# FFN up product of a hybrid decoder block: gate and up chunk computed together, block by block, in alternating pairs of PSUM banks

## What is computed

```python
def conv_ffn(xn, w_up, conv_w, conv_b, w_down):      # xn (1, 256, 2048), D_FF = 5632
    h = causal_dwconv(xn @ w_up, conv_w, conv_b)     # w_up (2048, 11264), 3 taps
    a, b = jnp.split(h, 2, axis=-1)                  # gate half, up half
    return (jax.nn.silu(a) * b) @ w_down             # w_down (5632, 2048)
```

## Time and profile before

| | |
|---|---|
| median of 3 runs | 1511.31 us (1510.9 to 1511.93) |
| the profiled execution's own time | 1510.21 us |
| its span, first to last instruction | 1508.4 us |
| mean granted clock of TensorE | 0.999 of full speed |
| PE matmuls busy | 1493.1 us (99%) |
| PE weight loads busy | 1280.1 us (85%) |
| DVE busy | 1076.9 us (71%) |
| ACT busy | 818.1 us (54%) |
| share of PE in the chain that ended last | 97% |
| weights and inputs read from HBM | 286.18 MB, 191 GB/s over the span |

### The profile page before, as it was taken

The page is one execution under the profiler, slowest core; times in us unless marked ns, Lnnn a source line. Parts: engine busy times, 40 slices in busy tenths (PEclk is TensorE's granted clock), DMA queues, the critical chain, the costliest instruction groups (busy, mean ns, idle before and its releaser), DMA issues.

```text
span 1508.4 us, 24165 instructions
## 1 busy us (share of the span) xinstructions
PE 1493.1 (99%) x7908; PEld 1280.1 (85%) x7908; DVE 1076.9 (71%) x1576; ACT 818.1 (54%) x1184; POOL 2.9 (0%) x9
## 2 busy tenths in 40 slices
PE   8999999999999999999999999999999999999997
PEld 6888888888888888888888888888888888888886
DVE  5756676788887556665568777777777777777876
ACT  5644478745555546544566454454545555454654
POOL 0000000000000000000000000000000000000000
PEclk9999999999999999999999999999999999999999
DMA  8756655665557554445546655655555556555554
GB/s 307 271 193 219 208 177 190 201 201 167 176 167 240 179 187 160 155 149 195 187 164 199 190 194 187 192 185 194 192 185 195 184 190 195 193 183 191 185 194 139
DMA packets 80314, 288.88 MB, mean 192 GB/s; under 512 B 8928, under 2 KB 10464, under 8 KB 79376
## 3 DMA queue, kind: packets, MB, share of 16 engines
q1 hardware_dynamic: 76320, 276.33, 56.0%
q10 hardware_dynamic: 3456, 8.64, 1.7%
q0 software_dynamic: 496, 3.34, 0.6%
HBM read 286.18 MB, written 2.10 MB: 191 GB/s over the span
## 4 chain that ended last, share of the span: by engine, by line
PE 97%; DVE 1%; ACT 1%; DMA 0%; issue 0%; SPq 0%; ACTq 0%; DVEq 0%
PE ps L261 96%; PE ps L318 0%; DMA raw<-in_stream 0%; DVE wlo L877 0%; ACT whi L527 0%; DVE vm L1354 0%; DVE xres L1364 0%; PE ps L390 0%; ACT scr L761 0%; ACT scr L854 0%; DVE sm_ L1223 0%; DVE xres L1327 0%; SPq L217 0%; DVE wlo L931 0%; ACT vm L867 0%
## 5 line engine op out<-in xcount | busy, mean ns | idle before, releaser
L261 PE MATMUL ps<-xT,whi 128*128 128x512 f32 x2304 | 727.5, 397 | 0.2
L877 DVE TENSOR_TENSOR wlo<-raw,whi 128x1024 fp32r<-128x1024 f32 x516 | 623.3, 1222 | 129.5 <-ACT whi L527 120.0
L527 ACT ACTIVATE whi<-raw 128x1024 fp32r<-128x1024 f32 x516 | 531.7, 1050 | 227.5 <-PE ps L261 220.9
L261 PEld LDWEIGHTS ps<-xT,wlo 128*128 128x128 f32 x2304 | 432.8, 188 | 102.1
L261 PE MATMUL ps<-whi,mixT 128*128 128x512 f32 x1472 | 461.1, 391 | 7.2 <-DVE wlo L935 5.8
L261 PE MATMUL ps<-xT,wlo 128*128 128x256 f32 x2304 | 453.0, 278 | 0.0
L261 PEld LDWEIGHTS ps<-xT,whi 128*128 128x128 f32 x2304 | 352.6, 189 | 2.3 <-DVE wlo L877 0.8
L261 PEld LDWEIGHTS ps<-whi,mixT 128*128 128x128 f32 x1472 | 277.3, 188 | 65.6 <-DVE mixT L926 5.8
L261 PE MATMUL ps<-wlo,mixT 128*128 128x512 f32 x736 | 287.2, 390 | 0.0
L542 ACT ACTIVATE hl<-ps 128x256 f32<-128x256 f32 x160 | 61.1, 382 | 236.7 <-PE ps L261 236.6
L895 DVE TENSOR_TENSOR tmp<-ps,hl 128x256 f32<-128x256 f32 x160 | 67.8, 424 | 146.1 <-ACT hl L542 145.8
(11 more groups left out here) (173 smaller groups left out, 637.4 us busy)
## 6 DMA issues: line engine op xcount, KB each, us to landing
raw<-in_stream SPq DMA_DIRECT2D x519, 512.0 KB, 3.4
xres<-in_xin ACTq DMA_DIRECT2D x2, 1024.0 KB, 6.9
scr<-in_xt_in ACTq DMA_DIRECT2D x8, 256.0 KB, 3.6
xres<-in_xin POOLq DMA_DIRECT2D x1, 2048.0 KB, 12.0
out_x<-vm SPq DMA_DIRECT2D x4, 512.0 KB, 3.1
kT<-in_memt_in SPq DMA_DIRECT2D x2, 512.0 KB, 8.7
vbuf<-in_memin ACTq DMA_DIRECT2D x1, 1024.0 KB, 9.4
gel<-in_memin ACTq DMA_DIRECT2D x1, 1024.0 KB, 7.4
```

The lines of the kernel that those rows point to most:

```text
L261: return nc.tensor.matmul(o, l, r, start=start, stop=stop, skip_group_check=True)
L527: A(whi[:, 2 * pr + s, :], raw[:, 2 * pr + s, :], ACT.Copy).then_inc(hi_done, 1)
L877: V.tensor_tensor(wlo[:, 2 * pr + s, :], raw[:, 2 * pr + s, :], f32(whi[:, 2 * pr + s, :]), ALU.subtract).then_inc(lo_done, 1)
```

## The change

The panels of a pair are laid out anew in the stream, so that slots 0 and 1 of its unit hold blocks kk = 0 to 7 of the gate chunk a and of the up chunk b, and slots 2 and 3 hold blocks 8 to 15 of a and b. PE goes through the blocks once for both chunks: at each kk it issues w_hi of a, w_hi of b, w_lo of a, w_lo of b against the same block of `xT`, and it waits for two panels at a time, before kk = 0 and before kk = 8. Pairs with even k accumulate in banks 4 and 5, those with odd k in banks 6 and 7. ACT and DVE now have nothing of the pair to do in the first of a unit's two steps; both copies, both sums and everything behind them are in the second. In the FFN's first pair `norm_tr(7)` stays at kk = 7, which is now late in the first half of the pair, and `row_of(2)` comes at kk = 13.

```diff
-            def up(m, n=2 * GF, at={}):
-                for j in range(n):
-                    narrow(m + j // 2, j % 2, xT, {} if j else at)
+            def up_pair(m, k, at={}):
+
+                for s in range(2):
+                    pe.wait_ge(lo_done, 4 * m + (2 * s + 2))
+                    for kk in range(8 * s, 8 * s + 8):
+                        if kk in at:
+                            at[kk]()
+                        w = slice(kk % 8 * P, (kk % 8 + 1) * P)
+                        for ab in range(2):
+                            mm(ps[:, 4 + 2 * (k % 2) + ab, :], whi[:, 2 * s + ab, w],
+                               xT[:, kk].rearrange("p a b -> p (a b)"), kk == 0, False)
+                        for ab in range(2):
+                            last = mm(ps[:, 4 + 2 * (k % 2) + ab, :T], wlo[:, 2 * s + ab, w], xT[:, kk, 0, :], False, kk == KT - 1)
+                            if kk % 8 == 7:
+                                last.then_inc(panels_used, 1)
...
-                    14: lambda: pe.wait_ge(nt_lo, 2 * KT)}
-            narrow(C_F // 2, 0, xT, NEXT)
-            narrow(C_F // 2, 1, xT, {7: lambda: row_of(2)})
-            up(C_F // 2 + 1, 2 * GF - 2)
+                    13: lambda: row_of(2), 14: lambda: pe.wait_ge(nt_lo, 2 * KT)}
+            up_pair(C_F // 2, 0, NEXT)
+            pe.wait_ge(row_read, 3)
+            for k in range(1, GF):
+                up_pair(C_F // 2 + k, k)
             with pe.Fori(1, NG - 1) as g:
                 m = C_F // 2 - 2 + 6 * g
-                up(m, 2)
+                up_pair(m, 0)
                 down(m + 1, g)
-                up(m + 3, 6)
-
-            up(NC // 2 - 8)
+                for k in range(1, GF):
+                    up_pair(m + 2 + k, k)
+
+            for k in range(GF):
+                up_pair(NC // 2 - 8 + k, k)
...
             def pair(m, g, k, hi_now, k0=0, also=None):
                 u, q = 8 * g + 2 * k, 4 * g + k
-                step(m, 0, lambda: copy_hl(0), lambda: last_tap(u, 0), lambda: (silu(q), also() if also else None))
-                step(m, 1, lambda: copy_hl(1), lambda: last_tap(u + 1, 1),
-                     (lambda: hidden_hi(q, k, k0)) if hi_now else None)
+
+                def both():
+                    for ab in range(2):
+                        A(hl[:, ab, :], ps[:, 4 + 2 * (k % 2) + ab, T:], ACT.Copy).then_inc(hl_copied, 1)
+
+                def rest():
+                    last_tap(u + 1, 1)
+                    silu(q)
+                    if hi_now:
+                        hidden_hi(q, k, k0)
+
+                step(m, 0, None, None, also)
+                step(m, 1, both, lambda: last_tap(u, 0), rest)
...
-            def up(u, ab, w):
-                ch.link(narrow_sum(w, ab, tmp[:, 5, :]))
-                V.tensor_tensor(tmp[:, ab, :], tmp[:, 5, :], row[:], ALU.mult).then_inc(up_ready, 1)
+            def up(u, ab, w, k):
+                dve.wait_ge(hl_copied, w + 1)
+                ch.link(V.tensor_tensor(tmp[:, 5 + ab, :], ps[:, 4 + 2 * (k % 2) + ab, :T], hl[:, ab, :], ALU.add))
+                V.tensor_tensor(tmp[:, ab, :], tmp[:, 5 + ab, :], row[:], ALU.mult).then_inc(up_ready, 1)
...
-                def up_a():
-                    if first:
-                        first()
-                    up(u, 0, w)
-
-                def b1():
+                def both():
+                    up(u, 0, w, k)
+                    up(u + 1, 1, w + 1, k)
+
+                def rest():
                     taps(u + 1, 1)
                     hidden(q, k)
-
-                step(m, 0, up_a, lambda: taps(u, 0))
-                step(m, 1, lambda: up(u + 1, 1, w + 1), b1, (lambda: hidden_lo(q, k, k0)) if lo_now else None)
+                    if lo_now:
+                        hidden_lo(q, k, k0)
+
+                step(m, 0, None, None, first)
+                step(m, 1, both, lambda: taps(u, 0), rest)
...
-    up = np.stack([up[:NF], up[NF:]], 1)
+    up = np.stack([up[:NF], up[NF:]], 1).reshape(NF, 2, P, 2, PAN).transpose(0, 3, 2, 1, 4).reshape(NF, 2, P, D)
```

## The result

The changed kernel takes **1521.38 us** (median of 4 runs, 1520.32 to 1521.81) against 1511.11 in the same comparison: 1.0068 times as long, 95% interval 1.0055 to 1.008. Forecast were 1520.3 us, between 1514 and 1527. The profiled execution took 1521.81 us with a span of 1520.0, against 1510.21 and 1508.4.

What follows compares the result with a forecast made beforehand. PE was taken to bound the kernel, waiting for nobody. Late panels (5.1 + 1.0) and the turn into the FFN (2.8) gave 8.9 us: 1519.1 on the profiled execution, median 1.1 higher, so 1520.3; 80% range 1514 to 1527.

Steps and rivals of the forecast that it cites:

- The pair's second step: ACT's and DVE's step behind a pair: slot 3 late by 0.19 us (loop) or 0.14 (written out); 5.1 plus 1.0 us.
- PE's own pace: PE's matmuls in the up product: 0 change taken, with bounds of 0.680 and 0.697 us a group.
- The rival that lives on them: Up product: repeating the moving operand in another bank brings groups to 0.680 us; total +1.7, 1513.0 us; chance 0.05.
- The second ladder: Chain from a pair's end to the next unit's slots 0 and 1: ready at 10.84, due 11.04, 0.20 us to spare.
- The turn: Entry into the FFN, first pair: PE stands 3.1 us once, 0.3 us is given back, net 2.8 us.
- The hole at slot 3: First FFN pair, before kk = 8: slot 3, split only after the last quarter's transposes, makes PE stand 3.1 us once.
- no wait before kk = 0: Sign for the FFN's pairs: PE does not wait for slots 0 and 1; waits there would make the prediction wrong.
- What was given back: First FFN pair: the wait ahead of `row_of(2)` goes, 0.3 us.
- The clock: Rival at the FFN's start: the 3.1 us hole brings the lower clock level, 2.4 us more, 1522.6 us; chance 0.07.
- that sign: Sign for PE: the profile's granted clock row still reads 1.00.
- The one that the Trainium skill has on cycling banks: Rival: the clock falls at each of the 34 small waits, some 80 us more; chance 1%.
- the 8.9: Sum of the forecast slowdown in us: 5.1 for loop waits, 1.0 for written-out waits, 2.8 net at the FFN's start.

## Why the prediction was right, and what it missed

**The pair's second step** carried the sum, and it holds row by row: the ladder, DVE's chain from the first copy to the end of slot 3's split, was forecast at 5.41 and measured 5.39; load 0.05 later; late 0.19 forecast and 0.18 measured in the loop, 0.14 and 0.14 where written out; 34 times, always where two pairs follow each other and never at a down chunk. Taking the lateness away took the time away, and adding 0.34 to it added 34 x 0.34. One reading is off by 0.01: the rows give 0.35 for the distance taken as 0.34, and 0.34 is what the new sums show.

**PE's own pace** was put at no change: 0.6968 us a group against 0.6965, and 0.6965 in the interleaved order once the waits are gone. Neither the bank nor the repeated moving operand matters. The rival that lives on them is gone, in the interleaved order and in the banks alone.

**The second ladder** was forecast at 10.84 and measured 10.80, its margin 0.20 and 0.23. It is as thin as stated: 0.03 is left with the taps moved (and -0.04 once), and -0.4 with the second sum moved.

**The turn** was half seen. The hole at slot 3 was 3.0 for 3.1. What failed is a step that the prediction didn't take: it asked of slots 2 and 3 when they are due, and of slots 0 and 1 only "no wait before kk = 0". But the row that it used for the length of the ladder, a split at 768.29 that ends at 769.52, is slot 1's of that same first pair, and the FFN starts at 768.71. It was there to be read: the FFN's first load starts at 768.49, the split would let it start at 769.57, 1.1 us late, and it came 1.14 late. In the kernel before, this panel was asked for only at 772.25. What was given back was 0.45 for 0.3.

**The clock** was a rival with 0.07 and came true in the profiled runs with holes of 2.3 and 3.0 us; the forecast proper had the clock at 1.00, and that sign failed in the first pair. The chance of 0.07 was too low for what all four profiled executions with a hole of 3.0 us then showed. In the changed kernel's the starts stand 0.43 apart for 3.4 us behind the hole, at a granted clock of 0.50, and cost 1.6 us. Its size was put at 2.4 from a start-up stretch of five us; the stretch was shorter. The rule that the Trainium skill has for it (TensorE: Matmul & The Clock Gate, section "HAM oscillation — how this bites in real kernels") is borne out by the trace for holes of 2.3 and 3.0 us (clock 0.83 over ten us), and not for those of 1.6 and 1.8 (1.00). The one that the Trainium skill has on cycling banks (the same page, section "A second HAM failure mode: psum-queue depth-cycling") is not borne out here: with small waits of 0.18 us and four banks by turns the loop's clock is 1.00.

Both omissions, 1.0 and 1.6 us, take the 8.9 to 11.5, and the small terms (waits 0.3 and hole 0.1 under the forecast, 0.15 more given back, 0.2 of pace) bring it to the 11.2 of the rest of the span. By the medians the difference is 10.3, so the forecast of 9.0 looks low by 1.3 only; executions of one kernel spread by 0.7 to 3.5 us, so that it is no more is luck. The range of 13 us was wide enough to hold both omissions.

## What to carry to other kernels

A consumer that takes two panels at once where it took them one by one moves the second one's due time forward by a panel's time, for every producer step that feeds it; go through all of them, the first of the stage and those of the stage before too. Work that is gathered into one step stands ahead of that step's splits: order a producer's list by who waits (splits first, taps later), and check the list's far end as well, where the same microseconds come back. If PE never waits, interleaving its matmuls buys nothing unless the pace itself changes, and the pace is seen in start distances, not in busy time.

## What the runs showed of the hardware

A wait of 0.2 us of PE leaves its busy time full: 550.00 of 550.00 us in both kernels, with 2928 and 2901 matmuls. The weight load behind a late split starts 0.05 us after it in the loop (0.11 before the FFN's first matmul), and a lateness of 0.18 is passed on in full; of 1.14 us PE made up 0.1. The 512-column matmuls keep 0.227 us in the down product and a group of 2 x 512 + 2 x 256 columns 0.697 in the up product whatever the bank order. PE's clock stayed at 1.00 behind holes of 1.6 and 1.8 us and went to the lower level for about 3.4 us behind holes of 2.3 and 3.0 us, in one profiled execution each of the first three lengths and in four kernels' at the last (the changed one, the taps moved, the second sum moved, one more operation). Executions of the same code part within the first 30 matmuls, by up to 2.8 us, and keep to 0.14 us of that distance for the next 750 us.
